# Expert blocks: the slot list fetched one block ahead, and expert 1's loads behind the first gather

## What is computed

```
expert_id = g_idx * EXPERTS_PER_GROUP + e_idx          # two experts per token
order = argsort(eid); tok_s = order // TOP_K           # rows sorted by expert
xbuf[dest] = xt[tok_s]                                 # blocks of 128 rows, one expert each
y_block = (silu(xb @ w_g[e]) * (xb @ w_u[e])) @ w_d[e]
out = h + segment_sum(ybuf[dest] * gate_s, tok_s)
```

## Time and profile before

| | |
|---|---|
| median of 3 runs | 2796.92 us (2794.7 to 2802.06) |
| profiled execution | 2790.89 us, span 2789.3 us |
| mean granted TensorE clock | 0.978 of 2.4 GHz |
| PE busy | 2625.4 us (94% of the span) |
| DVE, ACT, POOL busy | 1759.5, 1603.3, 738.2 us |
| chain that ended last | PE 72%, DMA 13% (8% the gathers, 4% the slot lists) |

### The profile page before, as it was taken

One profiled execution on the slowest core, in us unless ns is written; L12 is line 12 of the kernel. 1 busy time (PEld: TensorE's weight loads), 2 busy tenths in 40 slices (PEclk: granted clock), 3 DMA queues, 4 the chain that ended last, 5 costly groups with the idle time before them and its releaser, 6 DMA issues.

```text
span 2789.3 us, 48388 instructions
## 1 busy us (share of the span) xinstructions
PE 2625.4 (94%) x14283; PEld 1494.0 (54%) x14284; DVE 1759.5 (63%) x3598; ACT 1603.3 (57%) x2598; POOL 738.2 (26%) x826
## 2 busy tenths in 40 slices
PE   4999999999999999994799999999999999999997
PEld 1455555555555555552356555656555666665565
DVE  5677777777777777776545465555555555456552
ACT  7665555555655555554546576566656565566642
POOL 1132232322232322222232322222222222222321
PEclk9999999999999999997899999999999999999999
DMA  8376666666666666666665667666776656567743
GB/s 312 83 165 164 164 153 158 159 152 154 161 164 164 156 156 160 151 150 203 208 172 177 207 203 238 183 215 191 226 224 198 194 182 197 163 193 220 210 115 61
DMA packets 546411, 495.43 MB, mean 178 GB/s; under 512 B 411787, under 2 KB 411948, under 8 KB 545340
## 3 DMA queue, kind: packets, MB, share of 16 engines
q1 hardware_dynamic: 517516, 406.08, 51.3%
q0 software_dynamic: 28848, 88.77, 13.3%
HBM read 309.74 MB, written 87.88 MB: 143 GB/s over the span
## 4 chain that ended last, share of the span: by engine, by line
PE 72%; DMA 13%; DVE 5%; ACT 3%; issue 3%; POOL 1%; SPq 1%; POOLq 1%; ACTq 0%; DVEq 0%
PE psG L575 11%; PE psB L1725 9%; PE psA L1725 9%; DMA xg<-hn_rows,slots 8%; PE psE L575 6%; PE psF L575 6%; PE psD L575 6%; PE psC L575 6%; PE psF L1725 5%; PE psG L1725 5%; DMA slots<-slot_table 4%; PE psH L575 3%; DVE up_lo L1941 1%; PE psC L1733 1%; PE psD L1733 1%
## 5 line engine op out<-in xcount | busy, mean ns | idle before, releaser
L575 PE MATMUL psG<-wi_all,both_xT 128*128 128x512 f16 x1536 | 345.2, 381 | 11.2 <-DMA both_xT<-x 11.2
L575 PEld LDWEIGHTS psG<-wi_all,both_xT 128*128 128x128 f16 x1536 | 148.8, 98 | 188.4 <-DMA both_xT<-x 11.4
L1651 POOL DMA_INDIRECT xg<-hn_rows,slots x80 | 129.3, 1616 | 446.9 <-DMA slots<-slot_table 216.2
L1725 PE MATMUL psA<-gate_hi,gT_hi 128*128 128x512 f16 x632 | 241.0, 381 | 3.7 <-issue 2.0
L1725 PE MATMUL psB<-up_hi,gT_hi 128*128 128x512 f16 x632 | 240.5, 381 | 0.0
L1725 PE MATMUL psB<-up_lo,gT_hi 128*128 128x512 f16 x632 | 240.3, 380 | 0.0
L1725 PE MATMUL psB<-up_hi,gT_lo 128*128 128x512 f16 x632 | 240.3, 380 | 0.0
L1725 PE MATMUL psA<-gate_lo,gT_hi 128*128 128x512 f16 x632 | 240.0, 380 | 0.0
L1725 PE MATMUL psA<-gate_hi,gT_lo 128*128 128x512 f16 x632 | 240.0, 380 | 0.0
L1835 ACT ACTIVATE aT_hi<-psE 128x512 fp32r<-128x512 f32 x79 | 47.2, 597 | 321.8 <-PE psE L1740 321.8
L1803 ACT ACTIVATE up_hi<-wi_all 128x4096 bf16<-128x4096 f32 x62 | 224.2, 3617 | 0.2
(11 more groups left out here) (336 smaller groups left out, 5677.7 us busy)
## 6 DMA issues: line engine op xcount, KB each, us to landing
wi_all<-in_w_gate SPq DMA_DIRECT2D x32, 2048.0 KB, 10.0
wi_all<-in_w_up SPq DMA_DIRECT2D x32, 2048.0 KB, 10.9
wi_all<-in_w_down SPq DMA_DIRECT2D x32, 2048.0 KB, 8.9
xt<-in_x SPq DMA_DIRECT2D x32, 512.0 KB, 3.8
um<-u_rows SPq DMA_DIRECT2D x64, 256.0 KB, 2.7
out_rows<-h SPq DMA_DIRECT2D x32, 512.0 KB, 2.9
xres<-in_x SPq DMA_DIRECT2D x31, 512.0 KB, 4.6
hn_rows<-xres SPq DMA_DIRECT2D x31, 512.0 KB, 2.9
```

The lines of the kernel that those rows point to most:

```text
L575: m = nc.tensor.matmul(ps, left[:, l, k, :], weights.half(r, k, n, width), start=(k == opens and j == 0), stop=(k == closes and j == 2))
L1651: pool.indirect_dma_start(xg[:], None, hn_dram, bass.IndirectOffsetOnAxis(ap=slots[:, 0, 0:1], axis=0), bounds_check=SEQ + P - 1).then_inc ...
L1725: m = nc.tensor.matmul(ps[:, :], l[:, k, :], r[:, r_k[n], :], start=(n == 0 and j == 0), stop=(n == len(l_k) - 1 and j == 2))
```

## The change

Two things are changed.

1. The list of a block is fetched one block earlier into a tile of its own, `slots_next`, also across the border between two experts. In block b POOL now does `shift(b)`, then `renew(b)` (wait for the fetch issued in block b-1, one copy into place 0 of `slots`, waited for), then the fetch for block b+1, then the gather of block b. The experts on POOL have a walk of their own: the first block, a loop over the middle ones, the last block, whose fetch names the next expert. It reads a third number per expert, the count less one, from `blocks_of`, which is 32 columns wider. Block 1 goes through the general `scatter` instead of a small stand-in.
2. SP issues the loads of gate and up of expert 1 behind `mixed(sp)` and behind the landing of the first gathered rows.

```diff
 def sync(sp):
         sp.wait_ge(summed, 2)
+        mixed(sp)
+        sp.wait_ge(rows_in, 16)
         for n in SCALED:
             load_expert(sp, n, 1, 1)
-        mixed(sp)
 def gpsimd(pool):
+        def load_slots(e, i):
+            pool.dma_start(slots_next[:], table[bass.ds(e * CAP + i * P, P), :]).then_inc(slots_in, 16)
...
-        def block_(e, i, b, p, r, follow):
...
+        def renew(b):
+            pool.wait_ge(slots_in, 16 * (b + 1))
+            hold(pool, held)
+            g.tensor_copy(slots[:, 0, :], slots_next[:]).then_inc(renewed, 1)
+            pool.wait_ge(renewed, b + 1)
+            hold(pool, held)
+
+        def block_(b, follows):
...
                 shift(b)
-            pool.dma_start(slots[:, 0, :], table[bass.ds(e * CAP + i * P, P), :]).then_inc(slots_in, 16)
-            pool.wait_ge(slots_in, 16 * (b + 1))
-            if not (isinstance(b, int) and b == 0):
+            renew(b)
+            if follows is not None:
+                load_slots(*follows)
+            if not first:
                 pool.wait_ge(xgT_ps, 2 * b)
                 hold(pool, held)
             gather()
...
+        def expert(e):
+            n = pool.value_load(blocks_of[0:1, bass.ds(e, 1)], min_val=2, max_val=TILES)
+            base = pool.value_load(blocks_of[0:1, bass.ds(e + E, 1)], min_val=0, max_val=4 * TILES)
+            final = pool.value_load(blocks_of[0:1, bass.ds(e + 2 * E, 1)], min_val=1, max_val=TILES - 1)
+            start = 0 if is_zero(e) else base
+            block_(start, (e, 1))
+            with pool.If(n > 2):
+                with pool.Fori(1, final) as i:
+                    block_(start + i, (e, i + 1))
+            block_(start + final, None if isinstance(e, int) and e == E - 1 else (e + 1, 0))
+            return base + n
...
+        load_slots(0, 0)
+        expert(0)
+        with pool.Fori(1, E - 1) as e:
+            expert(e)
+        total = expert(E - 1)
```

More of the change, by code:

```diff
@@ L157, in build @@
         ident = cst[:, C_ID:C_ID + P]
-        blocks_of = ksb("blocks_of", [P, 2 * E], I32)
+        blocks_of = ksb("blocks_of", [P, 3 * E], I32)
         held = keep.enter_context(nc.semaphore("held"))
@@ L364, in mixer @@
     last = sig("last").sem
-    planned = 17
+    planned = 18
     LAST = TILES
@@ L1510, in vector @@
         step(v.tensor_scalar(blocks_of[:, counts], nb[:], float(P - 1), None, ALU.add))
-        step(v.tensor_scalar(blocks_of[:, E:], blocks_of[:, counts], 7, None, ALU.arith_shift_right))
-        step(v.tensor_scalar(blocks_of[:, counts], blocks_of[:, E:], 2, None, ALU.max))
+        step(v.tensor_scalar(blocks_of[:, E:2 * E], blocks_of[:, counts], 7, None, ALU.arith_shift_right))
+        step(v.tensor_scalar(blocks_of[:, counts], blocks_of[:, E:2 * E], 2, None, ALU.max))
         step(v.tensor_copy(nb[:], blocks_of[:, counts]))
@@ L1520, in vector @@
             shift *= 2
-        step(v.tensor_tensor(blocks_of[:, E:], ping[:], nb[:], ALU.subtract))
+        step(v.tensor_tensor(blocks_of[:, E:2 * E], ping[:], nb[:], ALU.subtract))
+        step(v.tensor_scalar(blocks_of[:, 2 * E:], nb[:], -1.0, None, ALU.add))
         assert steps[0] == planned
@@ L1557, in experts @@
     y = sb("y", [P, D])
+    slots_next = sb("slots_next", [P, 2], I32)
     ones, diagonal = sb("ones", [P, P], BF16), sb("diagonal", [P, 2 * P], BF16)
@@ L1589, in experts @@
     named = sem("named")
+    renewed = sem("renewed")
     SCALE_STEPS = 5
@@ L1673, in shift @@
             hold(pool, held)
-        def block_(e, i, b, p, r, follow):
-            known = isinstance(b, int)
-            if known and b == 0:
+        def renew(b):
[5 more added lines that the diff above has]
+        def block_(b, follows):
+            first = isinstance(b, int) and b == 0
+            if first:
                 pool.sem_inc(moved, 1)
@@ L1688, in block_ @@
             gather()
-            if known and b < 2:
+            if first:
                 pool.wait_ge(cleared, 3)
                 pool.sem_inc(named, 1)
-                pool.dma_start(out[SEQ + b:SEQ + b + 1, 0:8], y[0:1, 0:8]).then_inc(added, 16)
+                pool.dma_start(out[SEQ:SEQ + 1, 0:8], y[0:1, 0:8]).then_inc(added, 16)
             else:
@@ L1697, in block_ @@
             hold(pool, held)
-            if known and b == 1:
-                pool.wait_ge(added, 32)
+        def expert(e):
[9 more added lines that the diff above has]
+            return base + n
         pool.wait_ge(summed, 2)
@@ L1704, in gpsimd @@
         pool.wait_ge(cleared, 2)
-        total = walk(pool, block_)
+        load_slots(0, 0)
[3 more added lines that the diff above has]
+        total = expert(E - 1)
         shift(total)
```

## The result

The changed kernel takes 2726.4 us, the median of three executions (2725.52 to 2726.7), against 2798.2 us, the median of four executions (2794.7 to 2802.06) of the kernel before beside it. The ratio is 0.9742, with a 95% interval of 0.9723 to 0.9762: some 72 us faster. One further execution, of 2802.76 us at a mean clock of 0.935 instead of 0.983, is left out of this comparison. The forecast was 2733 us. The profiled execution took 2725.52 us, where the sum had 2726.4.

A forecast was written before the change was run, and what follows sets the result against it. PE bounds the expert stage at 17.23 us a block, stalled ten times by POOL's gather loop. From the median 2796.92, less 64.5 (61.9 for stalls, 2.6 for the start), came 2732.4, rounded to 2733 us; range 2722 to 2766.

The forecast's parts named there:

- the sum: Whole kernel: 2790.89 - 61.9 - 2.6 = 2726.4 us for an execution like the profiled one.
- ten stalls: Expert stage: ten PE waits of 4.0 to 4.4 us for gathered rows, with slowed matmuls behind; all go, -61.9 us.
- The loop: POOL's gather, shift, list fetch, next gather: 21.21 us against PE's 17.23 a block; the change makes it 15.8, quiet 12.9.
- a loop that is too slow uses up its slack: POOL's loop: slack of some 7 us is used up, then PE stalls, about each fourth or fifth block in two-block experts.
- (a): Expert stage: some stalls stay, POOL's copies held by DVE's splits and gathers delayed 1 to 2 us; 2757 us, chance 0.10.
- (d): POOL's queue: the fetch in front delays each gather by more than it saved, so slower; 2862 us, chance 0.07.
- (b): Expert stage: a new bound appears, weights or ACT late in two-block experts; 2750 us, chance 0.06.
- (c): Expert stage: the list isn't what delays; the earlier gather meets the weight load and lands as before; 2794 us, chance 0.05.
- With the loop at 13 to 16 us POOL waits for PE ... lands ... 7 us early.: Expert stage: gather b is issued when PE has taken rows b-1, landing 9 to 10 us later, 7 us early.
- The start: First list and gather without expert 1's loads beside them: gather lands at 1330.3 instead of 1332.89, -2.6 us.
- The price of the loads: Expert 1's gate and up start 12.8 us later; taken as 0, with +4 us at block 1's psH stall in the range.
- From the profile to the median: Profiled execution was 6.0 us under its median; carried over: 2796.92 - 64.5 = 2732.4, rounded to 2733 us.

The follow-up runs named there:

- the kernel of the list alone: Changed kernel with SP's load order as before, so only the slot list is fetched a block ahead: 2734.17 us, 0.9778 of the kernel before.
- look-ahead inside an expert: Changed kernel, but the first block of each expert fetches its own list when needed: 2748.53 us, 0.9826 of the kernel before.
- the kernel with the loads alone: Kernel before, with only the loads of expert 1 moved behind the first gathered rows: 2790.54 us, 0.9975 of the kernel before.

## Why the prediction was right, and where not

**The stalls.** Right, and shown. The sum took 61.9 us for ten stalls; the 75 blocks became 63.4 us shorter, the pace being 17.21 and not 17.23. Taking the look-ahead out brings the stalls back, leaving it alone in keeps them away, the loads' place does nothing to them. That the sum for the profiled execution, 2726.4, is also the measured median to the digit is luck: its terms were off by 1.5 us for the stalls and 0.7 for the start, in opposite directions.

**The loop.** Right in its direction: the list's wait on POOL made the gathers late. Its size was taken from one long loop. There the list took 6.48 us, and the mean of all is 4.5. What goes in its place was put too high: from the shift's end to the next gather the sum has 0.83 + 2.0 = 2.8 us, as it counts the 0.83 twice, and the trace 2.2 (least and median). So the loop of the earlier trace rows lost some 6 us, not 5.4, and the mean one 3.9. And "a loop that is too slow uses up its slack" is only half of it: loops of 23 us stand in the undisturbed stretch too, followed by two of 12 to 16. The stalls came where a gather held back by `y` and a list was followed by a second loop of 17 to 22 us and a slow gather.

**The small costs.** Right: the copy 0.18 us at the median with single ones of 2.3; the fetch ahead does not delay the gather to be seen (longest landing 10.2 us); the third register load nothing, as four more of them per block cost nothing either. With that (a) and (d) fall: no stall of 4 us is left, and the added latency is far below the point at which (d) decides. (b) falls with 1290.80 us of 1290.80 busy; (c) with the kernel of the list alone.

**"With the loop at 13 to 16 us POOL waits for PE ... lands ... 7 us early."** This step was wrong in half of the blocks. Only 38 of 80 gathers wait for PE, and the 7 us early are 9.0 at the median but 3.9 at the least. I had written that the scatter stays hidden since it waits for `y`; it is this wait, 626.7 us in 79 blocks, that holds the gather queued behind it on POOL. The result did not hang on it, since behind `y` only the copies and the fetch's issue were left in the loop; my expectation for look-ahead inside an expert did, and missed by 16.5 us.

**The start.** The sum gave 2.6 us; from the first list's issue it was 3.1, and 1.9 against the profile before, whose first stage ended 1.2 us earlier. The price of the loads was rightly nothing. But 2.6 compares with a start before in which the gather was 2.8 us ahead of SP's third load; in the kernel of the list alone it is 0.85 us ahead, and the same edit is worth 8 us. That the lead decides it I read from the landings (9.57 us there, 5.63 before); no run varied the lead by itself. In the kernel with the loads alone the median fell by 6.4 us, while its profile shows a start shorter by 4.0 us (7.65 instead of 11.64) and 75 blocks longer by 2.3; what makes up the rest stays open.

**From the profile to the median.** This step made nearly the whole miss of 6.6 us. I carried the 6.0 us by which the profiled execution before lay under its median over to the changed kernel. That execution, at 2790.89 us, lies under all 35 others of the kernel before; the profiled one of the changed kernel lies 0.9 us under its median. Before, executions spread from 2791.2 to 2802.06 us; changed, from 2724.75 to 2730.34. If the spread comes largely from waits, it goes away with them, and the sum for the profiled execution, 2726.4, was the better forecast of the median too. That the stalls made the spread is inferred from these two spreads alone and not shown: the changed kernel has fewer executions (13), and the kernel with the loads alone, which keeps the stalls, spreads over 10 us through one execution and over 4 without it.

**Not tried:** a second tile for the gathered rows, which would take the loop apart altogether. It could bring nothing behind the first gather here, as PE has no other wait left for rows.

## What to carry to other kernels

Add up the loop that a waiting resource goes round in, issue to issue, and set it against the pace of the engine that bounds. Then look at each turn and not only at the mean: what counts is how long before its use a transfer lands in the tightest turn. Delay that stays under this lead costs nothing, and beyond it a few turns that are long one after the other cost more than the same time spread evenly. Dummy delay finds where the lead ends. Look for the last thing that the issuing engine waits for in that loop, whatever is queued ahead of the transfer, and not only at the buffer that the transfer needs; and make the dummy delay from something that touches no shared port. When one profiled execution lies at the edge of its spread, don't carry the distance between one execution and its median over to the new kernel.

## What the runs showed of the hardware

- A fill of SBUF on POOL held a DVE instruction of two columns until the fill ended: 2.19 and 4.80 us instead of 0.17. Register loads on POOL that add 2.7 us a block cost nothing (2726.83 us).
- A list of 1 KB landed after 2.17 us with the DMA engines free, and after 5.94 us beside two loads of 2 MB; a gather of 512 KB after 4.59 and 9.57 us, the latter with a third load issued 0.85 us behind it.
- SP's own issue of a weight load took 0.37 us at the start of the stage and 4.01 and 6.65 us for the third and fourth load behind the first gather. In the kernel with the loads alone these two took 3.93 and 0.88 us.
